# Both feed-forward blocks: six early tiles, alternating products, two more operand slots, block sums between the additions

## The chip, the cores and the metric

The kernel runs on one core of one Trainium2 chip. The metric is the device time of one execution in microseconds (us). TensorE (PE) does the matrix products, VectorE (DVE), ScalarE (ACT) and GpSimd (POOL) the elementwise work, and SyncE (SP) issues the DMAs. Each engine takes its instructions in a fixed order and waits on semaphores.

## What is computed

Two layers of an encoder over 1024 tokens of width 1024, in float32. Layer 0 mixes tokens by retention, layer 1 by neighbourhood attention, each beside attention into 256 memory tokens. Every layer ends with the same feed-forward block:

```python
for i in range(DEPTH):                      # DEPTH = 2
    a = rms_norm(h, norm_g[i, 0])
    y = retention_layer(...) if i == 0 else na_layer(...)
    h = h + rms_norm(y, norm_g[i, 1])
    a = rms_norm(h, norm_g[i, 2])
    gate, up = jnp.split(a @ ffn_w_in[i], 2, axis=-1)     # 1024 -> 2 x 2816
    f = (jax.nn.silu(gate) * up) @ ffn_w_out[i]           # 2816 -> 1024
    h = h + rms_norm(f, norm_g[i, 3])
```

## The kernel before, in words

**Arithmetic.** Every float32 operand is split into a high part (ScalarE writes it as float32r) and the rest (GpSimd or VectorE subtracts), and a product is three matmuls: high by high, high by rest, rest by high (`three`, lines 1979 to 1981). The feed-forward block uses the seven products of a Strassen-like scheme instead of eight, over the two halves of the input width, the two token halves, and gate against up.

**Input products.** The hidden width is 22 tiles j of 128. Each tile has seven products p, named "1" to "7", of 12 matmuls each, 154 products q in all (`products`, `in_product`). For the first `NPRE` = 5 tiles products 1 and 2 run early, before the second token half has been transposed, and 7, 6, 5, 4, 3 later; the other tiles run in the order 1, 6, 2, 7, 5, 4, 3. A weight operand of q is made by ScalarE (`operand_hi`) and GpSimd (`operand_lo`) in one of six slots OPS; GpSimd first makes four weight combinations for each tile (`combine`). The moving operands AOP are the activations, and sums of the two token halves.

**Banks.** Products 1 and 2 of a tile go to the same PSUM bank. ScalarE copies the result of 1 out, then 2 is added onto the bank, and ScalarE takes the silu of it (`gate_out`). VectorE adds the copy to 6, and goes on to 7, 5, 4 and 3 (`hidden_sums`, line 1562). It then multiplies silu and up and forms the sums that the output products need (`hidden_part`, lines 1578 to 1591).

**Second half at entry.** After four products TensorE transposes the second token half (`turn_second`, 32 transposes); ScalarE copies the first four pieces (`raw_second`, line 1068) and splits the last four (`hi_second`, line 1075), VectorE forms the sums and their low parts. At the same time the residual additions of these rows go on: VectorE adds (line 1486), ScalarE squares (977), GpSimd makes the factor (744, 745, 759, 761), VectorE scales (1437).

**Output products.** Seven times 11 products (`out_product`), each with a hidden operand loaded back from DRAM into six slots SRAW and a weight operand from BW (five blocks of 11 tiles). ScalarE splits both (`out_hi`, lines 1158 and 1163), VectorE makes the rest (`out_lo`, line 1599) and the weight sums (`block_sum`, line 1622). SyncE loads w2 in 1 MB parts (`load_w2`) and the hidden tiles (`load_s`), in one written order.

**Around it.** The last retention head (h = `RH`) overlaps with the first output projection. Between the layers `first_two` computes two units of the next projection, with the transposes of the last row tiles between them (line 2023), while the last residual additions of block 1 are finished; GpSimd splits the two weight units (line 732).

## Time and profile before

| | |
|---|---|
| timed runs, median | 2410.28 us (2410.07 to 2415.84, 3 runs) |
| profiled execution | 2411.24 us, span 2409.4 us |
| mean granted TensorE clock | 0.988 |
| PE busy | 2313.2 us (96%) |
| DVE, ACT, POOL busy | 1235.1, 933.0, 1037.0 us |
| DMA | 261.12 MB, mean 108 GB/s |

All times of the trace are on the axis of the span. A row of the timeline has the start, the duration, the engine, the line of the kernel, the operation and its tiles, and in brackets the idle time of the engine before it with what ended that. Durations of pipelined matmuls overlap; the distance between two starts is what one costs. In the page's slices by time PEclk is the granted clock of TensorE in tenths of full speed: 2.4 GHz is full, 1.2 GHz is half.

### The profile page before, as it was taken

Reading aid. Unit: us, or ns where it says so; the run is one execution under the profiler, and the core shown is the slowest. Engines: PE = TensorE matmul, PEld = TensorE weight load, DVE = VectorE, ACT = ScalarE, POOL = GpSimd, SP = SyncE. Lnnn points to the kernel's source line nnn. Section 1 sums busy time; section 2 is a strip of 40 time slices with the busy share of each in tenths; the row PEclk is TensorE's granted clock in tenths of the full one; section 3 lists DMA queues with packets and bytes.
Section 4 is the critical chain, followed back from the end, with each engine's and each line's share of the span. In section 5 each row is a group of like instructions: output and inputs, shape, how many; then the busy total and the mean of one; then the engine's idle time right before and its main releaser. Section 6 shows DMA issues by size and latency. Waiting matters only on the chain.

```text
span 2409.4 us, 31846 instructions
## 1 busy us (share of the span) xinstructions
PE 2313.2 (96%) x11752; PEld 1888.2 (78%) x11752; DVE 1235.1 (51%) x2107; ACT 933.0 (39%) x1851; POOL 1037.0 (43%) x775
## 2 busy tenths in 40 slices
PE   7999999998999999999989999989999999999998
PEld 6688888787788888788867777767777888887886
DVE  5644444637643434576753333345575434446767
ACT  5421211445232333344644444445552333323444
POOL 4123222367877777000342222212788777770001
PEclk9999999999999999999999999999999999999999
DMA  5121111342343222833521111122433323327334
GB/s 209 40 79 53 53 44 45 123 157 105 130 141 110 105 92 96 309 93 99 164 88 44 41 42 42 42 95 90 175 105 131 140 93 105 101 102 304 96 97 153
DMA packets 104231, 261.12 MB, mean 108 GB/s; under 512 B 22015, under 2 KB 22286, under 8 KB 102030
## 3 DMA queue, kind: packets, MB, share of 16 engines
q1 hardware_dynamic: 104078, 259.09, 31.6%
q8 instruction: 95, 1.56, 0.3%
q14 instruction: 58, 0.48, 0.1%
HBM read 193.77 MB, written 65.30 MB: 108 GB/s over the span
## 4 chain that ended last, share of the span: by engine, by line
PE 86%; DVE 3%; ACT 3%; issue 2%; DMA 1%; POOL 1%; SPq 0%; DVEq 0%; POOLq 0%; ACTq 0%
PE PS L1979 25%; PE PS L1981 25%; PE PS L1980 25%; PE PS L2221 3%; PE PS L2231 2%; PE PS L2460 2%; PE PS L2329 1%; DMA SRAW<-hidden_scratch 1%; PE PS L2411 1%; PE PS L2317 1%; PE PS L2257 1%; ACT qbd L1367 0%; PE PS L2340 0%; PE PS L2342 0%; PE PS L2341 0%
## 5 line engine op out<-in xcount | busy, mean ns | idle before, releaser
L1979 PE MATMUL PS<-AOP,OPS 128*128 128x512 f32 x1232 | 483.7, 393 | 23.2 <-DVE up L1562 8.9
L1980 PE MATMUL PS<-AOP,OPS 128*128 128x512 f32 x1232 | 482.2, 391 | 0.0
L1981 PE MATMUL PS<-AOP,OPS 128*128 128x512 f32 x1232 | 482.1, 391 | 0.0
L732 POOL TENSOR_TENSOR wlo<-stage,whi 128x1024 fp32r<-128x1024 f32 x82 | 199.8, 2442 | 516.1 <-ACT whi L958 515.8
L1979 PE MATMUL PS<-aT,whi 128*128 128x512 f32 (+1 forms) x768 | 337.0, 439 | 5.9 <-DVE aT L1449 4.4
L1981 PE MATMUL PS<-aT,wlo 128*128 128x512 f32 (+1 forms) x768 | 298.1, 388 | 0.0
L1980 PE MATMUL PS<-aT,whi 128*128 128x512 f32 (+1 forms) x768 | 297.4, 387 | 0.0
L1979 PEld LDWEIGHTS PS<-AOP,OPS 128*128 128x128 f32 x1232 | 233.0, 189 | 77.1 <-issue 19.6
L785 POOL TENSOR_TENSOR OPS<-TW,OPS 128x512 fp32r<-128x512 f32 x176 | 239.0, 1362 | 96.1 <-ACT OPS L1040 94.1
L1040 ACT ACTIVATE OPS<-TW 128x512 fp32r<-128x512 f32 x176 | 110.6, 633 | 416.9 <-POOL TW L809 374.6
L1981 PEld LDWEIGHTS PS<-AOP,OPS 128*128 128x128 f32 x1232 | 233.0, 189 | 48.9
L1980 PEld LDWEIGHTS PS<-AOP,OPS 128*128 128x128 f32 x1232 | 233.1, 189 | 48.0
L1979 PE MATMUL PS<-OPS 128*128 128x512 f32 x616 | 242.6, 394 | 9.3 <-DVE OPS L1599 7.5
L1980 PE MATMUL PS<-OPS 128*128 128x512 f32 x616 | 241.6, 392 | 0.0
L1981 PE MATMUL PS<-OPS 128*128 128x512 f32 x616 | 241.4, 392 | 0.0
L785 POOL TENSOR_TENSOR OPS<-stage,OPS 128x512 fp32r<-128x512 f32 x132 | 190.1, 1442 | 94.2 <-ACT OPS L1040 94.2
L744 POOL TENSOR_SCALAR msq<-sumsq 128x1 f32<-128x1 f32 x42 | 22.5, 537 | 375.5 <-ACT junk L977 373.8
L1562 DVE TENSOR_TENSOR up<-PS,u 128x512 f32<-128x512 f32 x88 | 60.9, 692 | 238.9 <-PE PS L1981 237.8
L1979 PEld LDWEIGHTS PS<-aT,whi 128*128 128x128 f32 x768 | 145.8, 190 | 47.0 <-issue 13.3
L1158 ACT ACTIVATE OPS<-SRAW 128x512 fp32r<-128x512 f32 x154 | 97.6, 634 | 216.3 <-PE PS L1981 199.4
L1980 PEld LDWEIGHTS PS<-aT,whi 128*128 128x128 f32 x768 | 145.7, 190 | 39.1 <-issue 7.7
L1981 PEld LDWEIGHTS PS<-aT,wlo 128*128 128x128 f32 x768 | 145.2, 189 | 30.5
(197 smaller groups left out, 3933.3 us busy)
## 6 DMA issues: line engine op xcount, KB each, us to landing
stage<-in_w SPq DMA_DIRECT2D x98, 512.0 KB, 3.5
stage<-in_wpack SPq DMA_DIRECT2D x82, 512.0 KB, 3.4
hidden_scratch<-HT SPq DMA_DIRECT2D x154, 256.0 KB, 2.1
SRAW<-hidden_scratch SPq DMA_DIRECT2D x154, 256.0 KB, 2.7
BW<-in_w SPq DMA_DIRECT2D x16, 1024.0 KB, 11.7
h_scratch<-Hb SPq DMA_DIRECT2D x24, 512.0 KB, 2.7
Hb<-h_scratch SPq DMA_DIRECT2D x24, 512.0 KB, 6.2
cat_scratch<-OC SPq DMA_DIRECT2D x14, 512.0 KB, 3.9
```

Of the source, the lines that this page charges most:

```text
L732: pool.tensor_tensor(wlo[:, slot, :], stage[:, slot, :], whi[:, slot, :].bitcast(F32), ALU.subtract)\
L785: pool.tensor_tensor(OPS[:, slot, 1, :], w1_operand(l, j, p), OPS[:, slot, 0, :].bitcast(F32), ALU.subtract)\
L1040: act.activation(OPS[:, OP_SLOT[l][q % SLOTS], 0, :], w1_operand(l, j, p), ACT.Copy).then_inc(o_hi, 1)
L1158: act.activation(OPS[:, s_op, 0, :], SRAW[:, s_slot(l, q), :], ACT.Copy).then_inc(g_hi, 1)
L1562: dve.tensor_tensor(dst, PS[:, in_bank(l, j, p), :], with_, ALU.add).then_inc(f_ed, 1)
L1979: pe.matmul(dst, stat[0], mov[0], start=start, stop=False, skip_group_check=onto)
L1980: pe.matmul(dst, stat[0], mov[1], start=False, stop=False, skip_group_check=onto)
L1981: return pe.matmul(dst, stat[1], mov[0], start=False, stop=stop, skip_group_check=onto)
L2221: pe.matmul(dst, stat, mov, start=True, stop=True).then_inc(s_mm, 1)
L2231: ins = pe.transpose(PS[0:keys, banks(r)[1], c * P:(c + 1) * P], SB[:, r % 3, c * width:c * width + keys], ident[:, :])
L2257: ins = pe.matmul(PS[64 * g:64 * g + 64, banks(r)[2], (r % 2) * P:(r % 2 + 1) * P], memV[:, kc, P * hp + 64 * g:P * hp + 64 * g + 64], PT[ ...
L2460: ins = pe.matmul(PS[half, 7, (q % 4) * GW:(q % 4 + 1) * GW], Vc[0:keys, place, half], PT[0:keys, r % 3, c * P + GW * b:c * P + GW * b + G ...
```

## The change

It changes both feed-forward blocks and three places around them. The number of matmuls is the same.

- `NPRE` is 6, and the twelve early products run in the order of `EARLY_IN`, so that product 2 of a tile does not directly follow its product 1, but for tile 5's neighbours. Product (0,"3") stands behind (1,"7"). Two early operands lie in a new tile OPX. The early results of tile 5 are kept in gB, and the gain rows for the end of the block are loaded later.
- `turn_second` runs after five products for row tiles 0 to 2, and after six for tile 3 and the last four pieces.
- VectorE's sums (`hidden_sum`) are called singly, with the parts of the tile before between them; `lo_second` and the low sum of "3" stand between the first sums.
- The operands of output products 0 and 1 are split before the last sums; loads of hidden tiles and of w2 alternate.
- Between the layers, the second weight unit is split behind the squares and the post factors.
- In the last retention head the key transposes go to banks 4 and 5, and three waits and a weight split move.

```diff
-OP_SLOT = ((1, 4, 2, 5, 0, 3), (2, 5, 0, 3, 1, 4))
-PAIR_AT = (0, 1)
+OP_SLOT = (1, 4, 2, 5, 0, 3)
+PAIR_AT = 2
-NPRE = 5
+NPRE = 6
+EARLY_IN = ((0, "1"), (1, "1"), (0, "2"), (1, "2"), (2, "1"), (2, "2"), (3, "1"), (4, "1"), (3, "2"), (5, "1"), (4, "2"), (5, "2"))
 def products():
-    early = [(j, p) for j in range(NPRE) for p in "12"]
-    return early + [(j, p) for j in range(KH) for p in (FIRST_ORDER if j < NPRE else ORDER)]
+    main = [(j, p) for j in range(KH) for p in (FIRST_ORDER if j < NPRE else ORDER)]
+    main.remove((0, "3"))
+    main.insert(main.index((1, "7")) + 1, (0, "3"))
+    return list(EARLY_IN) + main
...
+    OPX = at("OPX", [P, 2, 2, HALF], F32R, X + 104 * KB)
...
             def late_bank(l, k):
-            return 4 - D0[l] + (0, 1, 3, 2)[k]
+            return 4 - D0[l] + (0, 3, 2, 1)[k]
...
@@ SyncE, ffn @@
                 for q in range(4):
                     load_s(l, q)
-                for c in range(3):
-                    load_w2(l, 0, c)
+                load_w2(l, 0, 0)
                 load_s(l, 4)
                 load_s(l, 5)
-                for c in range(3):
-                    load_w2(l, 2, c)
-                for c in range(3):
-                    load_w2(l, 3, c)
+                load_w2(l, 0, 1)
+                load_s(l, 6)
+                load_w2(l, 0, 2)
+                load_s(l, 7)
+                load_w2(l, 2, 0)
+                load_s(l, 8)
+                load_w2(l, 3, 0)
                 store_hidden(l, KH - 1)
-                for q in range(6, N_OUT_FF):
+                for q in range(9, N_OUT_FF):
                     load_s(l, q)
-                    if q in (7, 9, 11):
-                        load_w2(l, 1, (q - 7) // 2)
+                    if q in (10, 12):
+                        load_w2(l, 2, q // 2 - 4)
+                        load_w2(l, 3, q // 2 - 4)
+                    if q in (14, 16, 18):
+                        load_w2(l, 1, (q - 14) // 2)
...
@@ GpSimd, out_phase @@
-                for p in "7564":
+                for p in "564":
                     combine(l, 0, p)
+                operand_lo(l, 2)
+                operand_lo(l, 3)
                 first_halves(s, 1)
...
                 pre_factor(s, 1, 1)
+                operand_lo(l, 4)
                 post_factor(s, 1, 3)
-                operand_lo(l, 2)
+                combine(l, 0, "7")
                 pre_factor(s, 1, 2)
-                operand_lo(l, 3)
+                operand_lo(l, 5)
                 pre_factor(s, 1, 3)
...
@@ GpSimd, end of ffn @@
                 if l == 0:
+                    los(U_NA + 1)
+                first_halves(1 + 2 * l, 1)
+                for i in range(TT):
+                    post_factor(1 + 2 * l, 1, i)
+                if l == 0:
                     los(U_NA + 2)
-                first_halves(1 + 2 * l, 1)
-                post(1 + 2 * l, 1)
+                    for i in range(TT):
+                        pre_factor(1, 1, i)
...
@@ ScalarE, out_phase, from the second square on @@
                 post_square(s, 1, 1, 1)
+                operand_hi(l, 4)
                 pre_square(s, 1, 0)
                 post_square(s, 1, 1, 2)
+                gate_out(l, 0)
+                operand_hi(l, 5)
                 pre_square(s, 1, 1)
                 post_square(s, 1, 1, 3)
-                operand_hi(l, 2)
+                gate_out(l, 1)
                 pre_square(s, 1, 2)
...
+                operand_hi(l, 7)
+                operand_hi(l, 8)
                 raw_second(l)
-                operand_hi(l, 7)
+                gate_out(l, 5)
                 hi_second(l)
...
@@ ScalarE, ffn @@
-                for q in range(10, N_IN_FF + 1):
-                    if q + 5 < N_IN_FF:
-                        operand_hi(l, q + 5)
-                    gate_out(l, q - 1)
+                for q in range(2 * NPRE, N_IN_FF):
+                    if q + 4 < N_IN_FF:
+                        operand_hi(l, q + 4)
+                    if q == QI[KH - 1, "4"]:
+                        out_hi(l, 0)
+                        out_hi(l, 1)
+                    gate_out(l, q)
...
@@ VectorE, ffn @@
                 turn_second(l)
-                for j in range(KH):
-                    hidden_sums(l, j)
-                    for part in range(3):
-                        if j < KH - 1:
-                            hidden_part(l, j, part)
+                hidden_sum(l, 0, "6")
+                hidden_sum(l, 0, "7")
+                lo_second(l)
+                hidden_sum(l, 0, "5")
+                lo_sum(l, "3", RAWA[:, 1, :, :], 4)
+                hidden_sum(l, 0, "4")
+                hidden_sum(l, 0, "3")
+                hidden_part(l, 0, 0)
+                for j in range(1, KH):
+                    for p, part in (("6", 0), ("7", 1), ("5", 2), ("4", 3), ("3", 0)):
+                        hidden_sum(l, j, p)
+                        if part:
+                            hidden_part(l, j - 1, part)
+                        if j == KH - 1 and p in "54":
+                            out_lo(l, "54".index(p))
+                    if j < KH - 1:
+                        hidden_part(l, j, 0)
...
@@ TensorE, turn_second and ffn @@
+                for i in tiles if part == 0 else ():
+                    pe.wait_ge(xs, tiles_before(t) + i + 1)
+                    for k in range(4):
+                        ins = pe.transpose(PS[:, D0[l] + k, i * P:(i + 1) * P], Y[:, i, k * P:(k + 1) * P], ident[:, :])
...
+                for k in range(4) if part else ():
+                    if k:
+                        pe.wait_ge(f_ea, gated(l, k - 1, 1))
...
                 for q in range(N_IN_FF):
-                    if q == 4:
-                        turn_second(l, 0)
+                    if q == 5:
+                        turn_second(l, 0, range(TT - 1))
+                    if q == 6:
+                        turn_second(l, 0, range(TT - 1, TT))
                         turn_second(l, 1)
                     in_product(l, q)
...
@@ TensorE, last retention head @@
+                k_bank = 4 if h == RH else 0
...
             chunk_scores(RH)
             out_rows(0, 0, 0, free=first_set_free(0))
-            out_rows(0, 0, 1, low)
             chunk_states(RH)
-            out_rows(0, 0, 1, high)
-            out_rows(0, 0, 2)
+            for k in range(1, 3):
+                out_rows(0, 0, k)
             chunk_outputs(RH)
             for k in range(3, 5):
                 out_rows(0, 0, k)
+            out_rows(0, 0, 5, low)
             turn_outputs(RH)
-            out_rows(0, 0, 5)
+            out_rows(0, 0, 5, high)
```

## Rows read from the trace of the kernel before

**Rows 1.** The page, busy time of TensorE: us, share of the span, instructions.

```profile
PE 2313.2 (96%) x11752; PEld 1888.2 (78%) x11752; DVE 1235.1 (51%) x2107; ACT 933.0 (39%) x1851; POOL 1037.0 (43%) x775
```

**Rows 2.** Windows: start:end and length, engines busy, clock, DMA share, GB/s; input products.

```profile
543.07:983.40 440.33, 428.49 (x1881) 352.48 (x1879) 208.20 (x218) 146.25 (x245) 330.35 (x248) 0.99 0.34 119
...
1741.50:2181.10 439.60, 427.70 (x1881) 351.93 (x1879) 208.24 (x218) 147.64 (x246) 330.75 (x248) 0.99 0.34 119
```

**Rows 3.** TensorE's waits, 543 to 984: us in total, times, longest us.

```profile
PE PS L1979 <- DVE up L1562: 4.5, 2, 2.7
PE PS L1979 <- issue: 3.9, 1, 3.9
PE PS L1979 <- ACT Hb L1053: 3.2, 4, 0.9
```

**Rows 4.** TensorE's waits, 984 to 1203 and 2182 to 2402, output products.

```profile
PE PS L1979 <- DVE OPS L1599: 3.7, 2, 2.0
...
PE PS L1979 <- DVE OPS L1599: 3.8, 2, 2.0
```

**Rows 5.** Timeline of TensorE, retention end and entry of the first block.

```profile
433.24 1.94 PE L2306 MATMUL PS<-ident,kT 128*128 128x128 f32 x8 [3.08 <-DVE OC L1885]
...
549.87 0.77 PE L1979 MATMUL PS<-AOP,OPS 128*128 128x512 f32 x1 [3.92 <-issue]
...
561.62 3.65 PE L2102 MATMUL PS<-ident,Y 128*128 128x128 f32 x32
...
622.89 0.47 PE L1979 MATMUL PS<-AOP,OPS 128*128 128x512 f32 x1 [2.67 <-DVE up L1562]
...
653.76 0.47 PE L1979 MATMUL PS<-AOP,OPS 128*128 128x512 f32 x1 [1.79 <-DVE up L1562]
```

**Rows 6.** Timeline of ScalarE, entry and passage of the first block.

```profile
555.28 0.60 ACT L1058 ACTIVATE sg<-PS 128x512 f32<-128x512 f32 x1 [2.07 <-PE PS L1981]
...
562.31 2.42 ACT L1068 ACTIVATE RAWB<-PS,gT 128x512 f32<-128x512 f32 x4
...
1002.99 0.63 ACT L1158 ACTIVATE OPS<-SRAW 128x512 fp32r<-128x512 f32 x1 [6.67 <-DMA SRAW<-hidden_scratch]
```

**Rows 7.** Timeline of VectorE, first block and layer passage.

```profile
554.71 1.77 DVE L1437 TENSOR_SCALAR Y<-Hb,rstd 128x1024 f32<-128x1024 f32 x1 [0.72 <-POOL rstd L745]
...
585.18 2.71 DVE L1549 SCALAR_TENSOR_TENSOR AOP<-PS,gT,AOP 128x512 fp32r<-128x512 f32 x4
...
619.70 1.65 DVE L1591 TENSOR_TENSOR HT<-HT 128x512 f32<-128x512 f32 x1
...
627.50 0.69 DVE L1562 TENSOR_TENSOR sg<-PS,u 128x512 f32<-128x512 f32 x1 [3.96 <-PE PS L1981]
...
656.79 0.69 DVE L1562 TENSOR_TENSOR sg<-PS,u 128x512 f32<-128x512 f32 x1 [2.37 <-PE PS L1981]
...
1204.25 2.38 DVE L1477 TENSOR_TENSOR Y<-Y,gB 128x512 f32<-128x512 f32 x1 [3.05 <-ACT junk L977]
```

**Rows 8.** Windows of 25 us at the two passages, columns as in rows 2.

```profile
975.00:1000.00 25.00, 23.01 (x95) 18.60 (x95) 13.96 (x22) 7.22 (x13) 0.00 (x0) 0.93 1.01 409
...
2200.00:2225.00 25.00, 23.14 (x95) 18.62 (x94) 18.96 (x31) 13.26 (x24) 0.00 (x0) 0.93 0.61 216
```

**Rows 9.** Timeline of SyncE's queue at the first block's passage.

```profile
977.74 4.00 SPq L590 DMA_DIRECT2D BW<-in_w  x6
```

**Rows 10.** TensorE's waits, 1190 to 1270, between the layers.

```profile
PE PS L2023 <- DVE Y L1437: 5.9, 4, 2.8
```

**Rows 11.** Timeline of GpSimd between the layers.

```profile
1203.69 2.40 POOL L732 TENSOR_TENSOR wlo<-stage,whi 128x1024 fp32r<-128x1024 f32 x1 [2.36 <-ACT whi L958]
```

**Rows 12.** TensorE's waits, 429 to 470, last retention head.

```profile
PE PS L2348 <- DVE ST L1873: 1.7, 1, 1.7
PE PS L2340 <- POOL qfb L897: 0.9, 1, 0.9
```

**Rows 13.** The chain of work in order of time, retention head before the last.

```profile
383.65 0.89 PE PS L2306 x8
```

253 lines of the change are left out of this document (137 added, 116 removed).

## The prediction

> **What bounds the kernel now.** I read first the page's busy times, then the windows by stage, then TensorE's waits stage by stage, and last the timelines of the queues around each wait. TensorE is busy 96% of the span [rows 1]: 2313.2 of 2409.4 us, so 96 us idle in all. The matmul count does not change (154 input products of 12 matmuls and 77 output products in each block, before and after), so the change can win only idle time and time at the half clock. In the first block's input products TensorE is idle 440.33 - 428.49 = 11.8 us, in the second block's 439.60 - 427.70 = 11.9 [rows 2]. Three kinds of wait make that up [rows 3]: 3.9 us once, 3.2 us in four waits on the ScalarE copy at L1053, 4.5 us in two waits on VectorE's sums. At the passage from input to output products two waits make 3.7 us in the first block and 3.8 in the second [rows 4].
>
> Idle time also costs clock. The product that starts at 549.87 after 3.92 us idle [rows 5] releases ScalarE at 555.28 [rows 6], 5.41 us later; the one at 622.89 after 2.67 us takes 4.61 us to 627.50; the one at 653.76 after 1.79 us takes 3.03 us to 656.79 [rows 5, 7]. So the half clock cost 2.4 and 1.6 us behind the two longer waits and nothing behind the 1.79 us one. At the full clock a product takes 2.73 us: the busy 428.49 us [rows 2] less 3.65 for the transposes [rows 5] and 4.0 for the half clock, over 1848 matmuls, times 12; the 3.03 has the start and the release on top.
>
> **The change part by part.** The profiled execution took 2411.24 us for a span of 2409.4; the median of the timed runs is 2410.28, 1 us less. I subtract from 2411.24 and take the 1 us off at the end.
>
> *1. Early products alternated, operands in two more slots.* Order was (0,1),(0,2),(1,1)...: product 2 of a tile adds into the bank from which ScalarE has just copied product 1, so TensorE waits for that copy: 3.2 us in four waits, and 3.9 us for tile 0, where the copy stood behind squares that waited for residual rows [rows 3]. Now another tile's product lies between, 2.73 us, which covers a 0.6 us copy, and gate_out(0) moves ahead of the third square. Both go: -7.1, and -2.4 for the clock.
>
> *2. Sixth early tile.* It moves two products ahead of the second half's sums; the total stays. TensorE reaches main product (0,7) when 12 instead of 10 products are done, while VectorE's sums of the second half keep their dates. Worth nothing by itself; its gain is that the other waits do not come back. It puts a second wait on the same path, though. The last four transposes (k=3) now go to bank 5, which product (2,2) has just filled, and whose silu stands on ScalarE behind raw_second. From the end of the tile-3 transposes ScalarE needs 2.42 us for four raw copies [rows 6], 0.5 us for the silu and 0.1 to start; TensorE has 12 transposes, 12 x 3.65/32 = 1.4 us [rows 5]. **New wait: 3.0 - 1.4 = 1.6 us.**
>
> *3. Sums taken singly between the additions.* hidden_part(odd tile) was five operations in a row of up to 1.7 us before the next tile's sums, and product 5 of the next tile found its bank or sum late: waits of 2.67 and 1.79 us [rows 5]. Now one part stands between two sums; a sum is 0.69 us, a part 1.65 [rows 7], a product 2.73, so VectorE keeps pace. -4.5, and -1.6 clock. But lo_second, once ahead of the sums, now stands behind sums 6 and 7 of tile 0: when (0,6) ends VectorE runs 2 x 0.69, 0.1, and 2.71 us [rows 7], 4.2 us, and product (0,4) wants it after one product, 2.73. **New wait: 1.5 us.** Queued behind it are sum 5 and lo_sum 3, wanted by (0,3) one product later than before, since (1,7) is now between; these are in time.
>
> *4. GpSimd and ScalarE order at entry.* The split of operand 4 stands on ScalarE behind a load issued only when operand_lo(3) is done, and the first residual square behind it; three 1.3 us GpSimd operations (combine 7, operand_lo 4 and 5) move between the norm factors. VectorE wrote the last row tile at 554.71 + 1.77 = 556.5 [rows 7]; by the queue dates it comes out about 2 us later, but TensorE needs it only after six products from 543 and twelve transposes (561) instead of after four. Cost 0; 0.3 us for product 0, whose last turned piece now ends after a residual addition that GpSimd releases later.
>
> So block 1's entry: -11.6 - 4.0 + 1.6 + 1.5 + 0.3 = **-12.2 us**. Block 2 has the same waits [rows 2]; I count its clock loss 0.8 less, as its half-clock stretches are shorter: **-11.4**.
>
> *5. Passage to the output products.* Operands 0 and 1 are split before the last sums instead of behind them; ScalarE is free then and the first 1 MB of w2 lands in time (asked for at the end of product 149, 11 us ahead). The first wait (2.0 us) goes. The second came from the load of hidden slot 6: six w2 loads were queued ahead at 977.74 [rows 9], and ScalarE waited 6.67 us for it [rows 6]. Now loads alternate, slot 6 is asked for at about 979. Cover: at 409 GB/s, 0.4 MB/us [rows 8], w2's middle parts follow the last hidden stores at about 995 and land about 1001, wanted about 1007. Clock: 0.93 of 25 us is 1.7 us lost, once in block 1 and twice in block 2 [rows 8]. **-3.7 - 1.7 = -5.4** and **-3.8 - 3.4 = -7.2**. SyncE's stores of the last hidden pair still hold back load 9; it has 10 us.
>
> *6. Between the layers.* TensorE waits 5.9 us for four row tiles [rows 10]. GpSimd's second weight split (2.40 us) [rows 11] and ScalarE's move behind the squares. The first gB multiplication took 2.38 us beside the split, where the sums of the same size take 0.69 [rows 7], and it held back the third output sum. Factors start some 4 us earlier; the split then lies in the residual additions, and its unit is wanted 5.4 us after the last output product, just in time. The load of the first unit is asked for two products later, when its slot is free for the split anyway 1 us after it can land; no cost, but little cover. Bounds +2 and -7; I take **-4**.
>
> *7. Last retention head.* Waits of 3.1 us [rows 5] and of 1.7 and 0.9 us [rows 12]; eight transposes took 1.94 us [rows 5] where those of the head before took 0.89 [rows 13], so the half clock costs twice that stretch's work, about 2.5 us over transposes and scores. Key transposes move to banks 4 and 5 and do not wait for gating: 16 transposes (1.8 us) run under the wait, leaving 1.3. The weight split leaves the way of the catT split, qfb is covered by out_rows 2, and half a row unit covers the last statistics. -1.8 - 2.5 - 0.9 - 1.4 = -6.6; bounds -3 (clock still falls) and -7.5; I take **-6**.
>
> Sum: 12.2 + 11.4 + 5.4 + 7.2 + 4 + 6 = 46.2; 2411.2 - 46.2 = 2365.0, 2364 beside the median; I say **2365**.
>
> **The rivals.** *A, GpSimd and VectorE block each other (0.20).* VectorE's 2.38 us multiplication started 0.56 us after the 2.40 us split and ended 0.5 after it [rows 7, 11]: it waited for all of it. If the moved GpSimd operations (three at each entry) each meet a residual addition, row tile 3 is 3.9 us later still, beyond its 2 us slack: 2 us and 1.6 us clock in each block, and the gain between the layers falls from 4 to 1. That makes 2365 + 7 + 3 = 2375. The Trainium skill, SBUF - State Buffer, section Who interferes with whom, has the rule: VectorE with two SBUF inputs and GpSimd reading SBUF hold a shared port exclusively, and the later one blocks. The trace agrees, by the rows just named.
>
> *B, the new waits drop the clock (0.15).* The 1.6 and 1.5 us lie just under the 1.79 that left the clock alone; the 1.86 us wait of block 2's passage was followed by a window at 0.93 [rows 8]. Four times 1.6 us: 2371; with A, 2382.
>
> *C, better than summed (0.08).* If VectorE's lo sums finish early and the late copies are quicker, or the layer passage gives 7: 2355.
>
> *D, slower (0.04).* ScalarE now splits operand q+4 in front of gate_out(q), before q+5 in front of gate_out(q-1): a split waits for the product before, so one product of lead (2.73 us) is lost. If hi split, combine and lo split then end after the product's start, every seven-product tile waits. There are 16 in each block; it decides from 46/32 = 1.4 us a tile; at 2 us a tile the kernel takes 2365 + 64 = 2429. Against it: a slot is free five products (13.6 us) ahead, and split 0.6, two combines 2.6, lo 1.3 and handovers 1 make 5.5 us.
>
> *E, it does not do what it says (0.03).* The new waits are as long as those removed, in every stage: 2408.
>
> **How the numbers follow.** The forecast case has 0.50 with its own range 2357 to 2371. The range that should hold 8 in 10 takes in A with B (2382), the unknown prices behind C (2351), and 4 us above A and B: 2351 to 2386. Some 0.3%, 7.2 us, is what a measurement tells from no change. Faster 0.93 (forecast, A, B, C), same 0.03 (E), slower 0.04 (D).
>
> **What would show it.** Right: no wait of TensorE on L1053 and none at 3.9 us in the entry; one of about 1.6 us before the last four transposes of the second half; one of 1.5 us before a matmul released by lo_second; no waits on HT or up sums; none on the OPS split at the output products' start; the layer passage idle under 5 us; first wait at the last head about 1.3 us. Wrong: transposes waiting on row tiles in the entry (A), half-clock stretches there (B), products waiting on GpSimd's OPS split in the steady tiles (D), the output products waiting on BW or SRAW loads.

## The result, and the profile after

The changed kernel takes 2376.82 us (median, 2375.16 to 2378.34, 4 runs) against 2410.18 us for the kernel before, timed beside it: a ratio of 0.9856, 95% interval 0.9844 to 0.9869, 33 us faster. The forecast was 2365 us, so 12 us of the gain are missing. The time lies in the forecast's range, but neither of the rivals that made the range that wide brought it there.

The page of the changed kernel, its span and the busy time of each engine:

```profile
span 2374.1 us, 31848 instructions
## 1 busy us (share of the span) xinstructions
PE 2298.8 (97%) x11752; PEld 1879.4 (79%) x11752; DVE 1241.5 (52%) x2107; ACT 926.3 (39%) x1851; POOL 1071.5 (45%) x775
```

TensorE's idle time fell from 96 us [rows 1] to 2374.1 - 2298.8 = 75 us, and its busy time by 14 us; the number of matmuls is the same, so that is time at the half clock. To see where, I cut both timelines of TensorE at the first and the last matmul of each stage (us):

| stage | before | after | difference | forecast |
|---|---|---|---|---|
| start to product 0 of block 1 | 543.07 | 537.78 | -5.3 | -6 + 0.3 |
| input products, block 1 | 440.08 | 426.68 | -13.4 | -12.5 |
| output products, block 1 | 220.04 | 221.17 | **+1.1** | -5.4 |
| from there to product 0 of block 2 | 538.32 | 537.30 | -1.0 | -4 |
| input products, block 2 | 439.28 | 426.70 | -12.6 | -11.4 |
| output products, block 2 | 218.23 | 214.03 | **-4.2** | -7.2 |

(The forecast's 0.3 us for product 0 falls ahead of it, so block 1 stands here at 12.2 + 0.3.) Both entries gave a little more than the sum said. The passages to the output products gave much less: 6.5 and 3.0 us are missing there, and 3.0 between the layers.

The windows of the input products, to set beside those before [rows 2]; the columns are the window, its length, TensorE's busy time, the granted clock and the DMA share:

```profile
537.78:964.46 426.68, 423.48 (x1880) 1.00 0.34 116
1722.93:2149.63 426.70, 423.51 (x1880) 1.00 0.35 116
```

TensorE's idle time is 3.2 us in each block, where it was 11.6 in both between the same two matmuls (the 11.8 and 11.9 of rows 2 have up to 0.3 us of the next wait in them), and the clock is full all through. All its waits there and right ahead of product 0, in block 1 (total, times, longest), are these:

```profile
PE PS L2039 <- DVE AOP L1599: 1.6, 1, 1.6
PE PS L2167 <- ACT Hb L1089: 1.4, 1, 1.4
PE PS L2039 <- DVE AOP L1494: 1.0, 1, 1.0
PE PS L2039 <- DVE up L1614: 0.2, 1, 0.2
```

L1599 is `lo_second` (forecast 1.5 us), L1089 the silu of product (2,2) ahead of the last four transposes (forecast 1.6), L1494 the last turned piece before product 0 (forecast 0.3). The waits on ScalarE's copies and the long ones on VectorE's sums [rows 3] are gone.

At the start of the output products there were two waits of up to 2.0 us [rows 4]. Now there is one, and it is longer. TensorE's timeline:

```profile
964.07 0.39 PE L2041 MATMUL PS<-AOP,OPS 128*128 128x512 f32 x1
968.95 0.80 PE L2039 MATMUL PS<-OPS 128*128 128x512 f32 x1 [4.49 <-DVE OPS L1646]
969.55 0.63 PE L2040 MATMUL PS<-OPS 128*128 128x512 f32 x1
...
973.39 0.52 PE L2040 MATMUL PS<-OPS 128*128 128x512 f32 x1
973.74 0.40 PE L2041 MATMUL PS<-OPS 128*128 128x512 f32 x1
973.98 0.39 PE L2039 MATMUL PS<-OPS 128*128 128x512 f32 x1
```

Starts lie 0.43 us apart until 973.4 and 0.23 us after: half clock (1.2 GHz) and full clock (2.4 GHz). The chain of waits through this place, in order of time (start, us, what; pieces under 0.05 us left out):

```profile
956.34 0.69 DVE up L1614
957.03 0.61 DVE HT L1630
957.66 1.93 DMA hidden_scratch<-HT
959.62 0.32 SPq L596
959.98 7.54 DMA BW<-in_w
967.54 0.64 ACT OPS L1201
968.21 0.70 DVE OPS L1646
968.95 0.80 PE PS L2039
```

It reads: sum 7 of the last tile (21), behind it part 1 of tile 20 (L1630), the store of that part, and only then SyncE's loads, the first 1 MB of w2 (`load_w2(0,0)`) among them, which lands after 7.54 us, 3.5 us after the last input product has started its last matmul. The 1.93 us in it are the landing of the store, and no load waits for that: four loads are issued from 958.15 on, half a microsecond behind the store, and the w2 part comes behind those four. SyncE's own queue:

```profile
949.76 8.21 SPq L587 DMA_DIRECT2D hidden_scratch<-HT  x2
958.15 1.78 SPq L596 DMA_DIRECT2D SRAW<-hidden_scratch  x4
959.98 0.43 SPq L602 DMA_DIRECT2D BW<-in_w  x1
```

The first row is the two stores of tile 20: one goes out at 949.76, the other only at 957.66, when part 1 is done. The w2 part does not need that store. It needs product 149 (counted from 0) to be done, which was so at 953.6, 6.4 us before it was asked for, but it stands behind the store in the queue. Block 2 has the same wait with 3.15 us:

```profile
2152.78 0.50 PE L2039 MATMUL PS<-OPS 128*128 128x512 f32 x1 [3.15 <-DVE OPS L1646]
```

This trace shows block 2 at its best. Three kernels of the experiments have the same code at the passage (early products in sequence, layers undone, key banks undone). Their waits there are 3.83, 4.15 and 3.71 us, the clock falls to half behind each, and the output products of block 2 take 217.08, 217.86 and 216.14 us instead of 214.03. So the -4.2 of the table is nearer to -0.4 to -2.1 in those executions.

### The profile page after: what moved, and what is told of

Its sections match the earlier page's. It is cut to its first block, busy times and chain, and to the rows that moved or that the text cites. A ratio compares the mean times of both kernels' runs of the same rounds, so it can differ in the third digit from the quotient of the medians.

```text
span 2374.1 us, 31848 instructions
## 1 busy us (share of the span) xinstructions
PE 2298.8 (97%) x11752; PEld 1879.4 (79%) x11752; DVE 1241.5 (52%) x2107; ACT 926.3 (39%) x1851; POOL 1071.5 (45%) x775
## 4 chain that ended last, share of the span: by engine, by line
PE 85%; ACT 3%; POOL 2%; DVE 2%; issue 2%; DMA 1%; SPq 0%; DVEq 0%; POOLq 0%; ACTq 0%
PE PS L2039 25%; PE PS L2041 25%; PE PS L2040 25%; PE PS L2288 3%; PE PS L2298 2%; PE PS L2530 2%; PE PS L2399 1%; POOL wlo L751 1%; PE PS L2481 1%; DMA BW<-in_w 1%; PE PS L2387 1%; PE PS L2324 1%; ACT qbd L1412 0%; POOL rstd L780 0%; PE PS L2411 0%
## 5 line engine op out<-in xcount | busy, mean ns | idle before, releaser
L2039 PE MATMUL PS<-AOP,OPS 128*128 128x512 f32 x1216 | 474.0, 390 | 5.4 <-DVE AOP L1599 3.2
L2041 PE MATMUL PS<-AOP,OPS 128*128 128x512 f32 x1216 | 473.2, 389 | 0.0
L2040 PE MATMUL PS<-AOP,OPS 128*128 128x512 f32 x1216 | 473.1, 389 | 0.0
L804 POOL TENSOR_TENSOR OPS<-TW,OPS 128x512 fp32r<-128x512 f32 x176 | 262.0, 1503 | 77.3 <-ACT OPS L1069 77.3
L2039 PEld LDWEIGHTS PS<-AOP,OPS 128*128 128x128 f32 x1216 | 228.3, 188 | 54.7 <-POOL OPS L804 4.0
L2041 PEld LDWEIGHTS PS<-AOP,OPS 128*128 128x128 f32 x1216 | 228.3, 188 | 47.5
L2040 PEld LDWEIGHTS PS<-AOP,OPS 128*128 128x128 f32 x1216 | 228.3, 188 | 47.1
L804 POOL TENSOR_TENSOR OPS<-stage,OPS 128x512 fp32r<-128x512 f32 x128 | 173.5, 1358 | 54.4 <-ACT OPS L1069 52.1
```

The source lines that it names most:

```text
L804: pool.tensor_tensor(place[:, 1, :], w1_operand(l, j, p), place[:, 0, :].bitcast(F32), ALU.subtract)\
L2039: pe.matmul(dst, stat[0], mov[0], start=start, stop=False, skip_group_check=onto)
L2040: pe.matmul(dst, stat[0], mov[1], start=False, stop=False, skip_group_check=onto)
L2041: return pe.matmul(dst, stat[1], mov[0], start=False, stop=stop, skip_group_check=onto)
```

## The experiments

Unless a text says otherwise, each is the changed kernel with one edit; 2376.82 us is what it stands against. All times are medians of four or five runs; the kernel before took 2409.99 to 2410.74 us beside them.

### Is it the store in front of the loads?

Part 1 of tile 20 runs ahead of the sums of tile 21:

```diff
-                        if part:
+                        if part and (j, part) != (KH - 1, 1):
                             hidden_part(l, j - 1, part)
...
                         hidden_part(l, j, 0)
+                    if j == KH - 2:
+                        hidden_part(l, j, 1)
```

> One edit on the changed kernel: VectorE's part 1 of hidden tile 20 runs right behind part 0 of that tile, ahead of sums 6 and 7 of tile 21 instead of behind them. Theory (the stores of the last even tile stand in SyncE's queue ahead of the loads of the output products' operands, and this part is what they wait for): the first block load of w2 is asked for about 6 us earlier, at the end of product 150, TensorE's waits of 4.49 and 3.15 us at the start of the output products go, and with the first also its 6.8 us at the half clock; 4.5 + 3.4 + 3.2 = 11, so 2366 us. Rival (the load itself is the limit: 1 MB that takes 7.5 us behind four loads of hidden slots): the load is asked for earlier but lands no sooner, and the waits stay at over 3 us; 2375 us or more. Second rival (both): the wait shrinks to 1 or 2 us in each block; 2370.

Measured: **2364.83 us** (2364.12 to 2365.46), ratio to before 0.9809 (0.9795 to 0.9824). Output products take 214.21 and 210.56 us instead of 221.17 and 214.03. Rows of VectorE and of SyncE's queue:

```profile
949.14 1.67 DVE L1630 TENSOR_TENSOR HT<-HT 128x512 f32<-128x512 f32 x1
951.33 1.79 SPq L596 DMA_DIRECT2D SRAW<-hidden_scratch  x4
953.16 0.43 SPq L602 DMA_DIRECT2D BW<-in_w  x1
```

The part runs 7.9 us earlier, the w2 load is asked for 6.8 us earlier, ScalarE has it at 959.76, and the only wait of TensorE left in the first 100 us of output products is one of 0.9 us much later. The theory holds, and both rivals fall. (The wait of 0.9 us was there before the change too.)

The other way round, the load moved and the part left late:

```diff
                 for j in range(KH):
...
+                    if j == KH - 1:
+                        load_w2(l, 0, 0)
                     if j:
                         store_hidden(l, j - 1)
...
-                load_w2(l, 0, 0)
```

> One edit on the changed kernel: SyncE asks for the first w2 block ahead of the stores of hidden tile 20, and all else stays, so part 1 of tile 20 is as late as in the changed kernel and so are the loads of hidden slots behind the stores. Theory (it is the w2 block behind the stores that makes the wait): it is asked for at the end of product 150, about 6 us earlier, and the first operands wait for the hidden slots only, which are in the changed kernel 3 us ahead of the block; the waits of 4.49 and 3.15 us shrink to under 1.5 us each; 2368 us. Rival (the hidden slots, which stay late, or the two kinds of load sharing the DMA engines, make the same wait): 2375 us, with ScalarE waiting on SRAW instead of BW.

Measured: **2364.27 us** (2363.03 to 2364.61), 4 us better than the 2368 expected. The w2 part is asked for at 952.03. ScalarE now waits for the hidden slots, but only until 960.98, and TensorE doesn't wait at all:

```profile
960.98 0.63 ACT L1197 ACTIVATE OPS<-SRAW 128x512 fp32r<-128x512 f32 x1 [8.34 <-DMA SRAW<-hidden_scratch]
961.52 0.62 ACT L1202 ACTIVATE OPS<-BW 128x512 fp32r<-128x512 f32 x1
```

TensorE reaches the output products at 962.9, and they take 214.61 and 210.61 us, 0.4 us more than with the first edit in block 1 and the same in block 2. So it was the w2 part behind the store that made the wait; the hidden slots behind it cost almost nothing.

And one step further in the wrong direction, the part behind sum 5 of tile 21:

```diff
-                        if part:
+                        if j == KH - 1 and part in (1, 2):
+                            if part == 2:
+                                hidden_part(l, j - 1, 1)
+                        elif part:
                             hidden_part(l, j - 1, part)
```

> One edit on the changed kernel, in the other direction than the first experiment: part 1 of hidden tile 20 runs behind sum 5 of tile 21, one product (2.7 us) later than in the changed kernel. Theory (this part, the store and the loads behind it are the chain of the passage's wait): the waits of 4.49 and 3.15 us grow by 2.7 us each, and the second may now bring the clock down (3 us): 2382 to 2386 us. Rival (the load's landing is set by the DMA engines, not by when it is asked for): 2377 us.

Measured: **2382.38 us** (2380.87 to 2383.3), at the lower end of what was expected. The waits are 8.25 and 6.82 us, 3.8 and 3.7 more than in the changed kernel where 2.7 was expected: SyncE needs 2.88 instead of 1.78 us for the four slot loads behind the store, and the w2 part is asked for at 963.63, 3.65 us later than in the changed kernel. The clock now falls in block 2 as well. Three positions of one VectorE operation of 0.6 to 1.7 us give 2365, 2377 and 2382 us.

### Was the order of the loads needed at all?

The first edit above, and the old order of the loads:

```diff
-                load_w2(l, 0, 0)
+                for c in range(3):
+                    load_w2(l, 0, c)
                 load_s(l, 4)
                 load_s(l, 5)
...
+                for c in range(3):
+                    load_w2(l, 2, c)
+                for c in range(3):
+                    load_w2(l, 3, c)
                 store_hidden(l, KH - 1)
-                for q in range(9, N_OUT_FF):
+                for q in range(6, N_OUT_FF):
```

> The changed kernel with part 1 of tile 20 early (2365 us), and SyncE's order of the loads at the passage as before the change: three w2 loads each time in a row, the last stores of hidden tiles behind them, hidden slot 6 behind these. Theory (the alternated loads are what took away the second wait of the passage, which came from the load of hidden slot 6): a wait of 1.7 to 2 us on SRAW returns some 15 us into the output products in each block, with 1.7 and 3.4 us of half clock behind it: 2 x 1.8 + 3.4 to 5.1 = 7 to 9 more, 2372 to 2374 us. Rival (with the operands split earlier and the last pair's sums singly the slot is asked for in time in either order): 2365 us.

Measured: **2381.93 us** (2379.61 to 2382.44), 17.1 more than with the alternated loads, twice what was expected. The wait is there, at product 6, for the load of slot 6, and its size is what I had wrong:

```profile
972.55 1.20 SPq L596 DMA_DIRECT2D SRAW<-hidden_scratch  x2
...
985.13 0.63 ACT L1191 ACTIVATE OPS<-SRAW 128x512 fp32r<-128x512 f32 x1 [11.71 <-DMA SRAW<-hidden_scratch]
...
987.14 0.79 PE L2036 MATMUL PS<-OPS 128*128 128x512 f32 x1 [6.75 <-DVE OPS L1641]
```

Slot 6 is at ScalarE 985.13 - 964.07 = 21.1 us after the end of the input products. In the kernel before it was 1002.99 - 983.15 = 19.8 us [rows 6]. The landing hardly moved; but before, TensorE came to product 6 late, by the first wait and the half clock behind it, about 3.7 us. With the first wait gone the second takes its place and more: the output products take 223.03 and 219.15 us in this run, against 220.04 and 218.23 in the kernel before. The two waits of a passage were one backlog of loads, and removing the first alone gives nothing.

### What each part at the entry is worth

The early products tile by tile (in the changed order tile 2, not tile 5, is the one whose product 2 follows its product 1 directly; the transposes of row tiles 0 to 2 lie between them):

```diff
-EARLY_IN = ((0, "1"), (1, "1"), (0, "2"), (1, "2"), (2, "1"), (2, "2"), (3, "1"), (4, "1"), ...
+EARLY_IN = ((0, "1"), (0, "2"), (1, "1"), (1, "2"), (2, "1"), (2, "2"), (3, "1"), (3, "2"), ...
```

> One part of the change undone: the twelve early products go tile by tile, product 1 and then product 2 of each, with six early tiles and the new operand slots as in the changed kernel. Theory (product 2 of a tile waits for ScalarE's copy out of its bank, 0.8 us each, and another tile's product between them is what hides it): five such waits in each block (for the third tile the transposes lie between), 4 us each, and in the first block up to 3 us more where the copy of tile 0 stands behind a square; the waits at the last four transposes and at the lo operations stay, and the clock may fall once in each block (2 us). 2385 to 2391 us. Rival (ScalarE's new order, with the copy of tile 0 ahead of the third square, did the work, and the short waits only use up slack that the later waits have): 2377 to 2379 us.

Measured: **2387.61 us** (2387.34 to 2391.37). The input products take 431.75 and 431.73 us, 5.1 and 5.0 more, which is 10.1 of the 10.8 us. The five waits are 0.73 to 0.87 us each (the third is put down to GpSimd's split), and the one for the copy of tile 0, 3.9 us before [rows 3], is 0.73. So ScalarE's order took away some 3.2 us of that wait, and the alternation the rest and all the others.

The sums of a tile in a row again, behind the parts of the tile before:

```diff
-                    for p, part in (("6", 0), ("7", 1), ("5", 2), ("4", 3), ("3", 0)):
+                    for part in range(1, 4):
+                        hidden_part(l, j - 1, part)
+                    for p in "67543":
                         hidden_sum(l, j, p)
-                        if part:
-                            hidden_part(l, j - 1, part)
```

> One edit on the changed kernel: VectorE does the three later parts of tile j-1 in a row and then the five sums of tile j, as before the change; the early tiles, the loads and the place of the second half's sums stay. Theory: the two kinds of wait are traded. The waits at the start of the output products (4.49 and 3.15 us, with 6.8 us at the half clock) go, as the last even tile's part runs early: -11 us. In the early stage products find their sums late again, up to 2.7 and 1.8 us in each block with 3 us of clock: +9 to +12. So 2375 to 2379 us. Rival (with the other tile's product between and a sixth early tile the sums have enough lead, and taking them singly was not needed): no such waits return, and the kernel takes 2366 us.

Measured: **2383.18 us** (2381.14 to 2383.58). Waits on VectorE's sums are back, three in each block instead of the two I counted; the second row is the 1.6 us that the changed kernel has too:

```profile
PE PS L2039 <- DVE up L1614: 7.0, 3, 2.5
PE PS L2039 <- DVE AOP L1599: 1.6, 1, 1.6
```

The input products take 8.8 and 10.3 us more, the output products 7.0 and 3.4 less. Both halves of the trade are there as the theory has them. The price at the input products, 19.1 us, is 7 above the upper end of what was expected, the time 4 above. The single sums are worth 19 us over the two blocks, and in the changed kernel they paid 10 of these back at the passage.

The two new waits of the entry, both removed, with the part of tile 20 early as well:

```diff
-                raw_second(l)
                 gate_out(l, 5)
+                raw_second(l)
...
+                lo_second(l)
                 hidden_sum(l, 0, "6")
                 hidden_sum(l, 0, "7")
-                lo_second(l)
```

> Three edits on the changed kernel: part 1 of tile 20 early as above; on ScalarE the silu of early product (2,2) ahead of the four copies of the second half, which wait for TensorE's transposes behind it; on VectorE the four lo operations of the second half ahead of sums 6 and 7 of tile 0. Theory: besides the 11 us of the passage, the wait of 1.36 us before the last four transposes and the one of 1.59 us before product (0,4) go, in both blocks: 2 x 2.9 = 5.9. So 2360 us. Rival (the lo operations in front make the sums late, and product (1,7) or (2,6) waits for its bank as long as (0,4) did; the silu in front holds up the copies for bank and operands): the entry keeps 2 to 3 us of waits in each block, 2366 us.

Measured: **2360.25 us** (2359.59 to 2361.75), ratio to before 0.9792 (0.9776 to 0.9809). Against the single edit's 2364.83 it is 4.6 us, where 5.9 were expected. The waits of the first entry are now:

```profile
PE PS L2041 <- POOL OPS L804: 1.2, 2, 0.9
PE PS L2041 <- DVE AOP L1494: 0.8, 1, 0.8
```

Both waits are gone, and GpSimd has become the latest in two places. Between the cuts the input products are shorter by 1.6 us in each block, 3.2 in all; the rest of the 4.6 lies where these edits change nothing (1.3 us between the layers in the two traces), so 3.2 us is what is shown for them.

### Between the layers

GpSimd and ScalarE in the order of before:

```diff
                 if l == 0:
-                    los(U_NA + 1)
+                    los(U_NA + 2)
...
                 if l == 0:
-                    his(U_NA + 1)
+                    his(U_NA + 2)
```

> One part of the change undone: between the layers GpSimd splits both weight units ahead of the norm factors and ScalarE makes the second hi part ahead of the squares, as before the change. Theory (the part is worth what the landmarks of the two traces show, 18.7 us from the last input-side work to the last transposes before and 16.4 after, since GpSimd's split now lies beside VectorE's residual additions and takes 3.04 instead of 2.40 us): 2.3 us are lost; 2379 us. Rival 1 (the part is worth the 4 us of the forecast, and something else there became worse): 2381 us. Rival 2 (it is worth nothing, and the shorter passage comes from elsewhere): 2377 us.

Measured: **2379.7 us** (2378.0 to 2382.16), 2.9 more. The cut between output products and product 0 of block 2 is 539.60 us here and 538.32 before. For the nine kernels whose code is the same as the changed kernel's in this stretch it is 534.45 to 537.30, mean 536.0. So this part is worth 2.3 us against the kernel before and 3.6 against this run, with a spread of 2.9 us among equal kernels, and the changed kernel's own trace, with 1.0, was at the poor end. Part of the gain and of the spread is the clock. In the 30 us behind the output products (window, length, busy, clock, DMA share, GB/s) the run with this part undone has 0.83, as the kernel before, the changed kernel 0.89, and seven of the other eight, the run with the key banks undone among them, 0.94:

```profile
1185.75:1215.75 30.00, 24.10 (x107) 0.83 0.40 137
...
1185.63:1215.63 30.00, 25.61 (x115) 0.89 0.43 139
...
1189.98:1219.98 30.00, 25.12 (x118) 0.94 0.43 138
```

The run's median has block 2's passage in it too, where its trace waits 4.15 us instead of 3.15. One reason why the forecast's 4 was too much can be seen in rows of GpSimd's and VectorE's timelines in the changed kernel:

```profile
1189.42 3.04 POOL L751 TENSOR_TENSOR wlo<-stage,whi 128x1024 fp32r<-128x1024 f32 x1
...
1187.76 2.48 DVE L1531 SCALAR_TENSOR_TENSOR Hb<-Y,rstd,Hb 128x1024 f32<-128x1024 f32 x2
1193.40 0.75 DVE L1482 TENSOR_SCALAR Y<-Hb,rstd 128x1024 f32<-128x1024 f32 x1 [3.17 <-POOL rstd L764]
```

The split takes 3.04 us where it took 2.40 [rows 11], since VectorE's second residual addition runs until 1190.2, and everything behind it on GpSimd waits: TensorE 1.44 us for this weight unit, VectorE 3.17 us for the first factor.

Two tries to do better, both on top of the three edits. First, VectorE makes the four residual additions in a row:

```diff
+                late = (s, th) == (1, 1)
                 for i in range(TT):
                     post_add(s, th, i)
-                    if s < 3 and i:
+                    if s < 3 and i and not late:
                         post_scale(s, th, i - 1)
                 if s < 3:
-                    post_scale(s, th, TT - 1)
+                    for i in range(0 if late else TT - 1, TT):
+                        post_scale(s, th, i)
```

> The kernel with all three edits (2360 us), and between the layers VectorE does the four residual additions in a row ahead of the four norm scalings, instead of one scaling behind each. Theory (residual additions 2 and 3, their squares and their factors stand behind the first scaling, which waits 3.2 us for GpSimd's factor, and that is what TensorE's last four groups of transposes wait for): row tiles 2 and 3 come 3 us sooner, TensorE's waits before the transposes (0.63, 2.01 and 0.51 us) and the half clock behind them go; 2356 us. Rival (VectorE's additions and GpSimd's weight split block each other): the split, 3.04 us beside two additions, takes 4 to 5 us beside four, TensorE's wait for it grows from 1.44 to about 3 us, the factors start later by as much, and nothing is won: 2359 to 2361 us.

Measured: **2361.01 us** (2359.64 to 2363.12): nothing won, as the rival has it, but not by its sizes. The split still takes 3.04 us and TensorE's wait for it is still 1.44; the one that is blocked is VectorE. Four additions take 6.98 us, where two take 2.48 (timelines of VectorE and GpSimd):

```profile
1178.84 6.98 DVE L1531 SCALAR_TENSOR_TENSOR Hb<-Y,rstd,Hb 128x1024 f32<-128x1024 f32 x4
1180.50 3.04 POOL L751 TENSOR_TENSOR wlo<-stage,whi 128x1024 fp32r<-128x1024 f32 x1
```

The split ends at 1183.54 and ScalarE takes the square of the third row tile only at 1184.66: VectorE's third addition waited for the whole split. The Trainium skill, SBUF - State Buffer, section Who interferes with whom, says that the one issued first holds the shared port for its whole instruction and that issue order decides who blocks; both rows agree (the split loses 0.64 us behind the second addition, the third addition about 2 us behind the split). TensorE's longest wait before the transposes falls from 2.0 to 0.8 us, but there are four now, 2.9 us in all where it was 3.1.

Second, VectorE makes this split itself, between its additions, and GpSimd leaves it out:

```diff
                     post_add(s, th, i)
+                    if (s, th, i) == (1, 1, 1):
+                        slot = w_slot(U_NA + 1)
+                        dve.wait_ge(w_hi, U_NA + 2)
+                        dve.tensor_tensor(wlo[:, slot, :], stage[:, slot, :], whi[:, slot, :].bitcast(F32), ALU.subtract)\
+                            .then_inc(w_lo, 1)
```

> The kernel with all three edits (2360 us), and the lo part of the second weight unit between the layers is made by VectorE, behind its second residual addition, instead of by GpSimd ahead of the norm factors. Theory (GpSimd's 3.04 us for this split and VectorE's additions block each other, which is why the row order changed in the run before won nothing): VectorE, which sits idle 3.2 us there, makes it in about 1.3 us; it is ready 1 us sooner, the first factor 2 us sooner, the last scaled row tile 2 us sooner; TensorE's four waits (1.44, 0.63, 2.01, 0.51 us) fall to about 2.5 us in all and the half clock behind them may go: 2356 to 2358 us. Rival (ScalarE's squares or VectorE's own order are the chain, not the blocking): the waits before the transposes stay, 2360 us.

Measured: **2360.02 us** (2359.04 to 2362.5), ratio to before 0.9795 (0.9782 to 0.9809), which can't be told from 2360.25. The local part of the theory holds in direction. The split takes 1.22 us, TensorE's wait for it falls from 1.44 to 0.35 us, and the four waits go from 4.6 to 3.1 us, where 2.5 was expected. But the longest of them, 2.0 us for row tile 2, is unchanged: its addition, square, factor and scaling follow each other over three engines, and its addition stands behind the scaling of tile 0. The stretch from the output products to product 0 of block 2 is 535.30 us against 535.62, so the blocking of the split is real but taking it away has won no time that these runs can show.

### GpSimd at the entry

All edits so far, and in the early tiles GpSimd makes the wanted operand between the two block combinations:

```diff
-                        if p == "7":
-                            combine(l, j, "7")
-                            combine(l, j, "5")
-                        elif p == "6":
-                            combine(l, j, "6")
-                            combine(l, j, "4")
+                        if p in "76":
+                            combine(l, j, p)
+                            operand_lo(l, q)
+                            combine(l, j, "54"["76".index(p)])
+                            continue
```

> The kernel with the three edits and VectorE's split between the layers, and one more: in the early tiles GpSimd makes the operand that TensorE wants next right behind the block combination that it comes from, ahead of the second combination (7, its operand, then 5; 6, its operand, then 4), instead of behind both. Theory (after the edits at the entry, TensorE waits 0.28 and 0.92 us for GpSimd's OPS in each block, since GpSimd's operations beside VectorE's long ones take 2.8 us where they take 1.3 alone): these waits go, 2 x 1.1 us; 2358 us. Rival (GpSimd is behind by its sum of work, not by its order): the waits stay or move to the operands of 5 and 4; 2360 us.

Measured: **2370.23 us** (2368.71 to 2371.7), 10 us worse, where neither the theory nor the rival had a loss. The input products take 4.7 us more in each block. The second combination had filled the time in which ScalarE makes the hi part. Now GpSimd idles in each of these places:

```profile
580.02 1.30 POOL L828 TENSOR_TENSOR TW<-stage 128x512 f32<-128x512 f32 x1
582.13 1.29 POOL L804 TENSOR_TENSOR OPS<-TW,OPS 128x512 fp32r<-128x512 f32 x1 [0.80 <-ACT OPS L1069]
```

TensorE's waits on these operands become 6.0 us in 14 places over both blocks. The rival, that GpSimd is behind by its sum of work, comes nearer to it: idle time given to it here is lost.

### The last retention head

Key transposes back to banks 0 and 1, waiting for the outputs of the head before:

```diff
-                if h == RH:
-                    pe.wait_ge(*EV[n - 2])
-                elif h >= 2:
+                if h >= 2:
                     pe.wait_ge(oc_rdy, h + 1)
...
-                k_bank = 4 if h == RH else 0
+                k_bank = 0
```

> One part of the change undone: the key transposes of the last retention head go back to banks 0 and 1, and so wait for the outputs of the head before, as all its other matmuls; the moved weight split, the row unit behind the outputs and the rest of this part stay. Theory (the other banks let 16 transposes, 1.8 us, run under VectorE's gating, and the rest of the wait is short enough to keep the clock): TensorE waits 3.1 instead of 1.25 us there and the clock falls behind it; 1.8 + 2.4 = 4.2 more, 2381 us. Rival (the transposes only moved the wait: what follows needs VectorE's outputs anyway and the time is the same): 2377 us.

Measured: **2380.87 us** (2377.57 to 2381.02). Product 0 starts at 542.10 instead of 537.78. TensorE waits 3.1 us instead of 1.2, and its clock in the window 425:450 is 0.86 instead of 1.00. The theory's 4.2 us stand against 4.3 at product 0. This is the bulk of this part's 5.3. (The 4.1 us of the medians agree, but partly by chance: in this trace block 2's output products take 2.1 us more, and the stretch between the layers 1.4 less.)

## Why the prediction was right or wrong

**Direction and most terms: right.** The steps at the entry (1 to 4) were to take 12.5 and 11.4 us from the input products and took 13.4 and 12.6. The two new waits were placed and sized well, 1.36 for 1.6 and 1.59 for 1.5. What was under-sized is the clock: I counted 4.0 us at the half clock in the entry from how late three products released somebody, and the busy time fell by 428.49 [rows 2] - 423.48 = 5.0; in block 2 I counted 3.2, and it was 427.70 - 423.51 = 4.2. The 0.3 us for product 0 was 0.98, 0.71 in most of the experiments. The retention head (step 7), with this wait in it, gave 5.3 for 5.7. In step 1, "another tile's product lies between" does not hold for tile 2; the transposes lie between there, and no wait for its copy shows.

**Step 5, the passage: wrong, and this is what the 12 us come from.** It said that the first w2 part "lands in time (asked for at the end of product 149, 11 us ahead)". It was asked for at 959.98, 4.5 us ahead of the end of the input products at 964.46. I had seen the stores of the last pair in SyncE's queue, and I had costed singly taken sums (step 3) at VectorE only. The step that failed is the link between them: `hidden_part(20, 1)` moved behind sum 7 of tile 21, its store waits for it, and the store stands ahead of the loads. Before, parts ran in a row behind their tile, and SyncE's queue of the kernel before has this store 15.8 us ahead of the end at 983.15, so that no wait told of it (the row is SyncE's two stores of tile 20):

```profile
967.39 1.04 SPq L575 DMA_DIRECT2D hidden_scratch<-HT  x2
```

In the changed kernel it goes out 6.8 us ahead of the end, and the w2 part is asked for behind it. The Trainium skill, DMA: Bandwidth & Descriptors, section Anatomy of one DMA — SWDGE (gpsimd) path, has it that a semaphore wait of a DMA is held on the issuing sequencer. The section is written for DMAs from GpSimd; SyncE's 8.21 us row above agrees for SyncE. In the cuts of the traces the passages fell short by 6.5 and 3.0 us; undoing the fault gives 12.0 us in the medians, as block 2's wait is mostly longer than in the changed kernel's trace. The run with the part early shows the rest of step 5 as forecast: output products 5.8 and 7.7 us shorter than before, for 5.4 and 7.2, and 2364.83 us in all for a forecast of 2365. That the two agree so closely owes something to errors that cancel: in that trace the entries are 2.0 us and the passages 0.9 us better than the sum, the layers 2.6 us worse.

**Step 6, between the layers: right mechanism, a size too large.** 2.3 to 3.6 us for 4, by the traces above, and 1.0 in the changed kernel's own. The bounds (+2 and -7) held it.

**The rivals.** *A* (GpSimd and VectorE block each other) exists: between the layers the split takes 3.04 us for 2.40. That this is all that step 6 lacks isn't shown, since taking the split away from GpSimd won nothing measurable. At the entry its condition was not met, as no transpose there waited for a row tile. Its 2375 us is near the result, but by another cause. *B* (the new waits drop the clock) is refuted: the clock is 1.00 over both entries. *C* (better than summed) holds for the entries, by 2.1 us, and nowhere else. *D* (one product of lead lost) is refuted: no product of a steady tile waits for GpSimd's operand in the changed kernel. *E* is refuted by every undone part. The mechanism that took the 12 us was no rival of mine. What the text named as a sign that it is wrong ("the output products waiting on BW or SRAW loads") is where it showed.

**What stays open.** The 1.0 us that undoing the key banks leaves of step 7 was not split further. The two edits at the entry were run together, not one by one. Why the first w2 part of block 2 lands up to 1 us later in some kernels with the same code wasn't looked into.

## What to carry to other kernels

When a step moves later on one engine, follow its result into the in-order queue that stores it, and list what stands behind that store. A load that needs neither is delayed all the same, and one hoisted ahead of it is a one-line repair. Two waits in a row on the same run of loads are one backlog: taking the first away moves its time to the second unless the loads change too. Fill the time of a handover with another piece of work, as the double combination does; an order by urgency alone can leave an engine idle that has no time to spare.

## What the runs showed of the hardware

The length of a wait does not settle whether the clock falls. Windows of ten microseconds that open at most 0.4 us ahead of the first matmul behind the wait (window, length, busy, clock, DMA share, GB/s); the kernel with the sums together, behind two waits of 2.52 us:

```profile
617.00:627.00 10.00, 9.67 (x43) 1.00 0.34 117
647.00:657.00 10.00, 9.67 (x36) 0.83 0.36 117
```

The changed kernel, behind 4.49 and 3.15 us:

```profile
968.90:978.90 10.00, 9.95 (x34) 0.76 0.97 351
2152.70:2162.70 10.00, 9.92 (x44) 1.00 1.02 408
```

Equal waits, and a fall to 1.2 GHz for part of the stretch in one case and none in the other; 3.15 us passed unharmed where 2.67 had not [rows 5]. Behind the transposes between the layers the granted clock differs (0.89 or 0.94 above) among kernels with equal code. A price for the clock from one row is a guess of some 2 us either way.

VectorE and GpSimd stretch each other at the entry too. In the changed kernel, where VectorE subtracts 128x2048 tiles while GpSimd splits operands:

```profile
565.50 3.38 DVE L1592 TENSOR_TENSOR AOP<-S3R,AOP 128x2048 fp32r<-128x2048 f32 x1
570.00 11.19 POOL L804 TENSOR_TENSOR OPS<-TW,OPS 128x512 fp32r<-128x512 f32 x4
```

The same subtraction takes 2.35 us at 585.97, another operation of this shape 2.29 (563.29), and the split 1.30 (561.69) against 11.19 / 4 = 2.8 here. And the 1 MB load took 7.54 us to land with seven 256 KB loads and two more w2 parts asked for between 958.15 and 962.9; the engines moved 351 GB/s in the window 960:985. At the same place with the part early it was at most 6.6 us, from 953.16 until ScalarE had it at 959.76.
